# Ten late value slots, dots written in place, earlier value gathers and other releases in a product-key expert layer

## Chip, core and metric

One Trainium2 core runs one decoder layer in one launch. The metric is device time in microseconds (us), median of several runs.

## What is computed

The layer is a hybrid mixer, a memory attention and a product-key expert network; the change touches the last part only.

```python
def peer_ffn(h, w_query, sub_keys, expert_u, expert_v):     # h: 256 tokens x 2048
    q = (h @ w_query).reshape(B, S, 8, 2, 128)
    scores = jnp.einsum('bshcd,hckd->bshck', q, sub_keys)    # 8 heads, 2 x 128 keys
    s_top, i_top = lax.top_k(scores, 16)                     # per half
    cand = s_top[..., 0, :, None] + s_top[..., 1, None, :]   # 16 x 16 pairs
    best, pos = lax.top_k(cand, 16)                          # 16 experts of 16384
    gate = softmax(best)
    act = gelu(einsum('ckd,cd->ck', expert_u[idx], x))       # a dot with each u row
    out = einsum('ck,ckd->cd', gate * act, expert_v[idx])    # weighted sum of v rows
```

The output is the root-mean-square norm of the sum, times `final_norm`. A row of `expert_u` or `expert_v` has 2048 float32, 8 KB.

## The kernel before

Up to about 740 us the kernel runs the mixer, the attention and the query product, weights split into high and low parts. The expert part then works in 16 groups of 128 tokens and one head (groups 0 to 7 are the first 128 tokens, 8 to 15 the second), 16 experts each, so that a gather brings one row to each of the 128 partitions (1 MB).

- **u gathers** (`gather_u`, L566, GpSimd's queue): gather n = 16 g + k. Four slots `u_ring` serve groups 0 and 1; from group 2 on there are seven, with `u_mid` (slots 4, 5) in the place of the query product's input and `u_high` (slot 6) in that of its output. Their first use waits for the last scores (`scores_ready`); later ones wait for the dot that used the slot.
- **Dots** (`dot_products`, L1373 and L1375, VectorE): two halves of 1024 elements each, product written to a bf16 scratch tile `product`, sum to `dots`. Before each stands a wait for the dot before it. Between the dots of group g VectorE does the routing of group g + 1 (`route_keys`, which first copies the scores to `cur`, `route_pairs`, `route_experts`) and, in groups 8 to 15, one-hot tiles for the scattered weights.
- **Value gathers of the first 128 tokens** (`first_values`, L573): 128 gathers v n in a ring of four slots, 4 behind group 1's u gathers, then 6 a group, 12 a group from group 8, 8 in the last two. TensorE takes them (`take_values`, L1875) with a diagonal of weights from ScalarE and counts `v_used`. The first take stands behind the last scores.
- **Dense tiles**: value rows of the upper 48 of 128 key blocks aren't gathered but multiplied from contiguous tiles of 1 MB (SyncE L503, slots 0 to 2 of `u_ring`; TensorE L1910, eight products for each half of the tokens per tile) with weights `wT` that one-hot products scatter (`scatter_weights`, L1904, `wT_done`). The last two heads' values are gathered whole, all others skip the rows that tiles hold. TensorE runs tile 0, then the last take of the first 128 tokens, which frees v slot 3, then tiles 1 to 47.
- **Late gathers** (L573): 128 value gathers m of the second 128 tokens, behind the last u gather on GpSimd's queue. `late_slot(m)` gives the slot: nine at first (7 = `late_first`, 8 = `late_third`, in the place later used by `final_gain`), then seven in turn. VectorE adds them up (`add_values`, L1407, counter `v_added`); six of the last 16 are left to TensorE (`take_late`, L1884), which comes to them after the tiles.

Each engine runs its queue in order, so a wait holds all that stands behind it. SyncE's queue holds the tiles, the load of `final_gain` after tile 8, and the output.

Of the kernel before, what the change touches and what calls it, by code (L numbers as in the profile page):

```python
# [33 lines left out]
def hybrid_layer(  # L34
# [8 lines left out]
    P = 128  # L43
# [13 lines left out]
    TOP = 16  # L57
# [99 lines left out]
    VS = 4  # L157
    V2S = 9
    late_first = put("late_first", [P, 1, D], F32, at_t2)
    late_third = put("late_third", [P, 1, D], F32, at_t1 + 24 * KB)  # L160
    wT = (put("wT0", [P, DENSE, P], F32, at_raw), put("wT1", [P, DENSE, P], F32, at_v))
# [3 lines left out]
    hotA = put("hotA", [P, 2, WB, P], F32, at_raw + 24 * KB)  # L165
    product = put("product", [P, D], BF16, at_f + 16 * KB)
    y_sum = put("y_sum", [P, TT, D], F32, at_t2)
# [27 lines left out]

    cur = put("cur", [P, 2, KEYS], F32, at_f + 8 * KB)
    rest = put("rest", [P, 2, KEYS], F32, at_f + 9 * KB)
# [27 lines left out]
    with ExitStack() as ctx:  # L225
# [108 lines left out]
        def v_slot(i):  # L334

            if i >= 7:
                return (late_first, late_third)[i - 7][:, 0, :]
            return v_parts[i // 2][:, i % 2, :]
# [65 lines left out]

        AT_FIRST = (7, 6, 0, 1, 2, 8, 4, 5, 3)
        IN_TURN = (6, 0, 1, 2, 4, 5, 3)

        def late_slot(m):

            return AT_FIRST[m] if m < V2S else IN_TURN[(m - V2S) % len(IN_TURN)]  # L410

# [19 lines left out]
        def _(sp):  # L431
# [66 lines left out]
            for t in range(DENSE):  # L498
                if t < 3:
                    sp.wait_ge(dot_done, last_dot(t) + 1)  # L500
                else:
                    sp.wait_ge(tile_used, t - 2)
                sp.dma_start(u_ring[:, t % 3, :], v_rows[(FROM + t) * KEYS:(FROM + t + 1) * KEYS, :]).then_inc(tile_landed[t % 3], 16)  # L503
                if t == 8:
                    sp.wait_ge(v_added, added_before(AT_FIRST.index(8) + 1))
                    sp.dma_start(final_gain[:, :], final_norm.rearrange("(o d) -> o d", o=1).to_broadcast([P, D])).then_inc(fgain_landed, 16)
# [10 lines left out]
        def _(pool):  # L517
# [40 lines left out]
            def gather_u(p, k):  # L558

                n = p * TOP + k  # L560
                before = u_before(n)
                if before is not None:
                    pool.wait_ge(dot_done, before + 1)
                elif n >= 2 * TOP:
                    pool.wait_ge(scores_ready, ITEMS["peer"][1])
                nc.gpsimd.indirect_dma_start(  # L566
                    out=u_slot(n), out_offset=None, in_=u_rows,
                    in_offset=bass.IndirectOffsetOnAxis(ap=idx[:, p, k:k + 1], axis=0)).then_inc(u_landed[u_index(n)], 16)
# [20 lines left out]

            pool.wait_ge(routed, 2)  # L590
            for k in range(TOP):
                gather_u(1, k)
            for n in v_share(1):
                first_values(n)
            for p in range(2, GROUPS):
# [6 lines left out]
            for m in range(TILE0):  # L602
                slot, before = late_slot(m), late_before(m)
                if before is not None and by_pe(before):
                    pool.wait_ge(v_used, late_turn(before) + 1)
                elif before is not None:
                    pool.wait_ge(v_added, added_before(before + 1))
                elif slot < VS:
                    pool.wait_ge(v_used, TILE0 - VS + slot + 1)
                elif slot in (4, 5):  # L610
                    pool.wait_ge(dot_done, GROUPS * TOP)
                else:

                    pool.wait_ge(dot_done, last_dot({6: 6, 7: 4, 8: 3}[slot]) + 1)
# [352 lines left out]
        def _(dve):  # L967
# [329 lines left out]
            def route_keys(g):  # L1297

                c, head = g // PH, g % PH
                step(nc.vector.tensor_copy(cur[:, :, :], scores[:, c, head * (2 * KEYS):(head + 1) * (2 * KEYS)].rearrange("p (a k) -> p a k", a=2)),  # L1300
                     apart=True)
                top16([(cur[:, a, :], rest[:, a, :], top[:, a, :], top_at[:, a, :]) for a in range(2)])

# [61 lines left out]

            def dot_products(g, q, c, ks, first=False):
                for k in ks:
                    n = g * TOP + k
                    dve.wait_ge(u_landed[u_index(n)], 16 * u_turn(n))
                    if not (first and k == 0):  # L1370

                        dve.wait_ge(dot_done, n)
                    nc.vector.tensor_tensor_reduce(out=product[:, 0:D // 2], in0=u_slot(n)[:, 0:D // 2], in1=hn[:, c, 0:D // 2], scale=1.0, scalar=0.0,  # L1373
                                                   op0=ALU.mult, op1=ALU.add, accum_out=dots[:, q, 0, k:k + 1])
                    nc.vector.tensor_tensor_reduce(out=product[:, D // 2:], in0=u_slot(n)[:, D // 2:], in1=hn[:, c, D // 2:], scale=1.0, scalar=0.0,  # L1375
                                                   op0=ALU.mult, op1=ALU.add, accum_out=dots[:, q, 1, k:k + 1]).then_inc(dot_done, 1)
# [83 lines left out]
            route(0)  # L1460
            dot_products(0, 0, 0, range(0, 4), first=True)
            gates(0)
# [514 lines left out]
```

## Time and profile before

| | before |
|---|---|
| median of 3 runs | 2032.69 us (2030.73 to 2033.88) |
| profiled execution | 2036.65 us, its span 2034.7 us |
| busy: TensorE, VectorE, ScalarE, GpSimd | 1781, 1369, 573, 1022 us |
| moved by the software queue (gathers) | 451 MB |
| moved by the hardware queue (weights, tiles) | 195 MB |

Shares over the whole span mix two unlike parts: the dense layers, bound by TensorE, and the expert part. The DMA share is the mean busy share of the core's 16 DMA engines; it can read slightly over 1. Idle time before an operation, in brackets or behind the bar, names what ended it.

### The profile page before, as it was taken

What the parts mean: (1) busy time and instruction counts of PE and PEld (TensorE: products, weight loads), DVE (VectorE), ACT (ScalarE), POOL (GpSimd) and SP (SyncE); (2) the same over time, 40 slices, a digit from 0 to 9 for tenths busy, and PEclk for the clock granted to TensorE, in tenths of its full rate; (3) what the DMA queues carried; (4) which work ended last, traced back from release to release, by engine and by line L of the source; (5) the groups of instructions that cost most, each with busy time, mean ns of one, the idle gap of its engine ahead of it and who ended that gap; (6) DMA issues with size and microseconds to landing.
All of it is one profiled execution on the core that took longest, in us unless ns stands there. A gap on an engine that the chain in (4) does not pass through costs nothing.

```text
span 2034.7 us, 19053 instructions
## 1 busy us (share of the span) xinstructions
PE 1781.4 (88%) x6299; PEld 1126.9 (55%) x6299; DVE 1369.4 (67%) x2205; ACT 573.4 (28%) x1039; POOL 1022.3 (50%) x643
## 2 busy tenths in 40 slices
PE   7999999999999999765655588888887999999996
PEld 6888888888888898522222233344433544444442
DVE  5463453223333348799999988787888887887866
ACT  5345454345443510110011033223314720000001
POOL 4443343444432413466566555564555746776743
PEclk9999999999999999887888899999998989999998
DMA  8986455665546689899999999999999999999997
GB/s 212 241 176 139 151 188 156 190 192 186 171 132 215 190 300 382 328 421 417 416 418 417 413 404 388 412 412 406 403 412 400 392 346 405 382 406 378 387 421 319
DMA packets 157643, 647.29 MB, mean 318 GB/s; under 512 B 25894, under 2 KB 31086, under 8 KB 95598
## 3 DMA queue, kind: packets, MB, share of 16 engines
q0 software_dynamic: 73728, 450.98, 55.0%
q1 hardware_dynamic: 83824, 195.16, 30.7%
q8 instruction: 50, 0.82, 0.2%
q14 instruction: 41, 0.34, 0.0%
HBM read 729.91 MB, written 2.10 MB: 360 GB/s over the span
## 4 chain that ended last, share of the span: by engine, by line
PE 38%; DMA 29%; DVE 19%; issue 7%; POOL 6%; SPq 0%; DVEq 0%; ACT 0%; POOLq 0%
PE acc L1526 10%; PE acc L1528 10%; PE acc L1527 10%; DMA u_ring<-in_peer_u_dram,idx 7%; DMA v_high<-in_peer_v_dram,idx 7%; DVE product L1373 6%; DVE product L1375 6%; DMA v_low<-in_peer_v_dram,idx 6%; DMA v_last<-in_peer_v_dram,idx 5%; PE misc L1875 3%; DVE y_sum L1407 2%; POOL v_high L573 2%; POOL v_low L573 1%; DMA late_first<-in_peer_v_dram,idx 1%; DMA u_mid<-in_peer_u_dram,idx 1%
## 5 line engine op out<-in xcount | busy, mean ns | idle before, releaser
L526 POOL TENSOR_TENSOR w_lo<-raw,w_hi 128x1024 fp32r<-128x1024 f32 x112 | 274.7, 2453 | 424.3 <-ACT w_hi L626 424.0
L1875 PE MATMUL misc<-v_high,diag 128*128 128x512 f32 x512 | 267.8, 673 | 99.4 <-DMA v_high<-in_peer_v_dram,idx 93.4
L1526 PE MATMUL acc<-w_hi,t_hi 128*128 128x512 f32 x896 | 354.7, 396 | 0.0
L1875 PE MATMUL misc<-v_low,diag 128*128 128x512 f32 x512 | 269.3, 678 | 93.3 <-DMA v_low<-in_peer_v_dram,idx 81.3
L1528 PE MATMUL acc<-w_hi,t_lo 128*128 128x512 f32 x896 | 349.3, 390 | 0.0
L1527 PE MATMUL acc<-w_lo,t_hi 128*128 128x512 f32 x896 | 348.7, 389 | 0.0
L974 DVE TENSOR_TENSOR w_lo<-raw,w_hi 128x1024 fp32r<-128x1024 f32 x112 | 152.7, 1363 | 267.1 <-ACT w_hi L626 266.9
L626 ACT ACTIVATE w_hi<-raw 128x1024 fp32r<-128x1024 f32 x224 | 237.0, 1060 | 330.7 <-PE acc L1528 290.2
L566 POOL DMA_INDIRECT u_ring<-in_peer_u_dram,idx x160 | 211.4, 1321 | 196.6 <-DVE dots L1375 139.4
L1373 DVE CUSTOM_DVE_ANT_0 product<-u_ring,hn 128x1024 bf16<-128x1024 f32 x160 | 196.0, 1225 | 70.0 <-DMA u_ring<-in_peer_u_dram,idx 53.8
L1875 PEld LDWEIGHTS misc<-v_low,diag 128*128 128x128 f32 x512 | 106.2, 216 | 246.6 <-issue 127.0
L1875 PEld LDWEIGHTS misc<-v_high,diag 128*128 128x128 f32 x512 | 105.2, 215 | 246.8 <-DMA v_high<-in_peer_v_dram,idx 124.0
L573 POOL DMA_INDIRECT v_low<-in_peer_v_dram,idx x100 | 150.9, 1509 | 113.0 <-PE misc L1875 70.4
L573 POOL DMA_INDIRECT v_high<-in_peer_v_dram,idx x100 | 144.1, 1441 | 120.4 <-PE misc L1875 75.0
L1375 DVE CUSTOM_DVE_ANT_0 product<-u_ring,hn 128x1024 bf16<-128x1024 f32 x160 | 195.6, 1223 | 0.0
L1528 PEld LDWEIGHTS acc<-w_hi,t_lo 128*128 128x128 f32 x896 | 168.2, 188 | 35.8
L1526 PEld LDWEIGHTS acc<-w_hi,t_hi 128*128 128x128 f32 x896 | 168.3, 188 | 33.9
L1527 PEld LDWEIGHTS acc<-w_lo,t_hi 128*128 128x128 f32 x896 | 168.4, 188 | 33.4
L1910 PE MATMUL misc<-u_ring,wT 128*128 128x512 f32 x384 | 176.7, 604 | 2.9 <-DMA u_ring<-in_peer_v_dram 2.3
L1910 PE MATMUL acc<-u_ring,wT 128*128 128x512 f32 x384 | 172.3, 592 | 0.0
L1910 PEld LDWEIGHTS misc<-u_ring,wT 128*128 128x128 f32 x384 | 74.1, 194 | 97.5 <-issue 92.9
L1910 PEld LDWEIGHTS acc<-u_ring,wT 128*128 128x128 f32 x384 | 73.0, 190 | 91.8 <-issue 91.8
(271 smaller groups left out, 2127.4 us busy)
## 6 DMA issues: line engine op xcount, KB each, us to landing
u_ring<-in_peer_v_dram SPq DMA_DIRECT2D x48, 1024.0 KB, 8.9
raw<-in_w_in_dram SPq DMA_DIRECT2D x64, 512.0 KB, 6.9
raw<-in_xattn_wk_dram SPq DMA_DIRECT2D x32, 512.0 KB, 4.7
raw<-in_xattn_wv_dram SPq DMA_DIRECT2D x32, 512.0 KB, 3.9
raw<-in_w_out_dram SPq DMA_DIRECT2D x32, 512.0 KB, 4.5
raw<-in_xattn_wq_dram SPq DMA_DIRECT2D x32, 512.0 KB, 4.7
raw<-in_xattn_wo_dram SPq DMA_DIRECT2D x32, 512.0 KB, 4.9
praw<-in_peer_wq_dram SPq DMA_DIRECT2D x24, 512.0 KB, 7.1
```

Of the source, the lines that this page charges most:

```text
L526: nc.gpsimd.tensor_tensor(w_lo[:, j % RING, :, :], raw[:, j % RING, :, :], w_hi[:, j % RING, :, :].bitcast(F32), ALU.subtract).then_inc(lo ...
L566: nc.gpsimd.indirect_dma_start(out=u_slot(n), out_offset=None, in_=u_rows, in_offset=bass.IndirectOffsetOnAxis(ap=idx[:, p, k:k + 1], axis ...
L573: nc.gpsimd.indirect_dma_start(out=v_slot(slot), out_offset=None, in_=v_rows, in_offset=bass.IndirectOffsetOnAxis(ap=idx[:, n // TOP, n % ...
L626: nc.scalar.activation(w_hi[:, j % RING, :, :], raw[:, j % RING, :, :], ACT.Copy).then_inc(hi_done, 1)
L974: nc.vector.tensor_tensor(w_lo[:, j % RING, :, :], raw[:, j % RING, :, :], w_hi[:, j % RING, :, :].bitcast(F32), ALU.subtract).then_inc(lo ...
L1373: nc.vector.tensor_tensor_reduce(out=product[:, 0:D // 2], in0=u_slot(n)[:, 0:D // 2], in1=hn[:, c, 0:D // 2], scale=1.0, scalar=0.0, op0= ...
L1375: nc.vector.tensor_tensor_reduce(out=product[:, D // 2:], in0=u_slot(n)[:, D // 2:], in1=hn[:, c, D // 2:], scale=1.0, scalar=0.0, op0=ALU ...
L1526: nc.tensor.matmul(o, xh, w_hi[:, s, kk, :], start=first, stop=False)
L1527: nc.tensor.matmul(o, xh, w_lo[:, s, kk, :], start=False, stop=False)
L1528: ins = nc.tensor.matmul(o, xl, w_hi[:, s, kk, :], start=False, stop=last)
L1875: ins = nc.tensor.matmul(o, diag[:, n % 4, :], v_slot(n % VS)[:, i * CW:(i + 1) * CW], start=False, stop=False)
L1910: ins = nc.tensor.matmul(o, wT[c][:, t, :], u_ring[:, t % 3, i * CW:(i + 1) * CW], start=c == 1 and t == 0, stop=c == 0 and t == DENSE - 1)
```

## The change

Seven edits:

1. A tenth late slot, `late_hot`, in the place of `hotA`, free once the last weights are scattered. The first 12 late gathers follow one order, the next 80 run through ten slots, the last 36 through seven.
2. SyncE waits for all 256 dots before tiles 1 and 2 (tile 0 as before), and loads `final_gain` after tile 40, once slot 8 is used for the last time (late sum 86).
3. The first uses of u slots 4 and 5 wait for the last query chunk read by TensorE in place of the last scores.
4. The first four value gathers stand before u gathers 9, 12 and 15 of group 1 in place of behind them.
5. The copy of the scores to `cur` is gone.
6. A dot writes its products as float32 over the u row that it reads.
7. The wait for the dot before stands only in groups 13 to 15.

```diff
@@ tiles
     VS = 4
-    V2S = 9
-    late_first = put("late_first", [P, 1, D], F32, at_t2)
-    late_third = put("late_third", [P, 1, D], F32, at_t1 + 24 * KB)
+    V2S = 10
+    late_more = (put("late_first", [P, 1, D], F32, at_t2), put("late_third", [P, 1, D], F32, at_t1 + 24 * KB),
+                 put("late_hot", [P, 1, D], F32, at_raw + 24 * KB))
-    product = put("product", [P, D], BF16, at_f + 16 * KB)
-    cur = put("cur", [P, 2, KEYS], F32, at_f + 8 * KB)
@@ order of the late slots
-        AT_FIRST = (7, 6, 0, 1, 2, 8, 4, 5, 3)
-        IN_TURN = (6, 0, 1, 2, 4, 5, 3)
+        AT_FIRST = (7, 6, 0, 1, 2, 9, 8, 4, 5, 7, 6, 0)
+        WIDE_TURN = (3, 1, 2, 9, 8, 4, 5, 7, 6, 0)
+        IN_TURN = (3, 1, 2, 4, 5, 6, 0)
+        NARROW = len(AT_FIRST) + 8 * len(WIDE_TURN)
         def late_slot(m):
-            return AT_FIRST[m] if m < V2S else IN_TURN[(m - V2S) % len(IN_TURN)]
+            if m < len(AT_FIRST):
+                return AT_FIRST[m]
+            if m < NARROW:
+                return WIDE_TURN[(m - len(AT_FIRST)) % len(WIDE_TURN)]
+            return IN_TURN[(m - NARROW) % len(IN_TURN)]
@@ SyncE, dense tiles
                 if t < 3:
-                    sp.wait_ge(dot_done, last_dot(t) + 1)
+                    sp.wait_ge(dot_done, last_dot(t) + 1 if t == 0 else GROUPS * TOP)
...
-                if t == 8:
-                    sp.wait_ge(v_added, added_before(AT_FIRST.index(8) + 1))
+                if t == 40:
+                    sp.wait_ge(v_added, added_before(max(m for m in range(TILE0) if late_slot(m) == 8) + 1))
                     sp.dma_start(final_gain[:, :], ...)
@@ GpSimd, gather_u
                     pool.wait_ge(dot_done, before + 1)
+                elif u_index(n) in (4, 5):
+                    pool.wait_ge(peer_used, PC)
                 elif n >= 2 * TOP:
                     pool.wait_ge(scores_ready, ITEMS["peer"][1])
@@ GpSimd, group 1
             for k in range(TOP):
+                if k == 9:
+                    first_values(0)
+                elif k == 12:
+                    first_values(1)
+                elif k == TOP - 1:
+                    first_values(2)
+                    first_values(3)
                 gather_u(1, k)
-            for n in v_share(1):
-                first_values(n)
@@ GpSimd, late gathers
                 elif slot in (4, 5):
                     pool.wait_ge(dot_done, GROUPS * TOP)
+                elif slot == 9:
+                    pool.wait_ge(wT_done, 2 * BATCHES)
@@ VectorE, route_keys
-                step(nc.vector.tensor_copy(cur[:, :, :], scores[...]), apart=True)
-                top16([(cur[:, a, :], rest[:, a, :], top[:, a, :], top_at[:, a, :]) for a in range(2)])
+                top16([(scores[:, c, (2 * head + a) * KEYS:(2 * head + a + 1) * KEYS], rest[:, a, :], top[:, a, :], top_at[:, a, :]) for a in range(2)])
@@ VectorE, dot_products
-                    if not (first and k == 0):
+                    if g >= GROUPS - WHOLE - 1:
                         dve.wait_ge(dot_done, n)
-                    nc.vector.tensor_tensor_reduce(out=product[:, 0:D // 2], in0=u_slot(n)[:, 0:D // 2], ...)
-                    nc.vector.tensor_tensor_reduce(out=product[:, D // 2:], in0=u_slot(n)[:, D // 2:], ...).then_inc(dot_done, 1)
+                    nc.vector.tensor_tensor_reduce(out=row[:, 0:D // 2], in0=row[:, 0:D // 2], ...)
+                    nc.vector.tensor_tensor_reduce(out=row[:, D // 2:], in0=row[:, D // 2:], ...).then_inc(dot_done, 1)
```

## Rows read from the trace of the kernel before

**Rows 1.** Page, DMA queues: packets, MB, share of 16 engines
```profile
q0 software_dynamic: 73728, 450.98, 55.0%
```

**Rows 2.** Windows: us, PE, PEld, DVE, ACT, POOL busy, PEclk, DMA share, GB/s
```profile
785.00:860.00 75.00, 60.28 (x280) 51.14 (x279) 64.44 (x135) 12.37 (x21) 37.99 (x27) 0.89 0.91 335
870.00:880.00 10.00, 5.34 (x12) 1.82 (x10) 8.86 (x30) 0.00 (x0) 6.25 (x7) 0.97 1.02 422
...
855.00:1165.00 310.00, 186.98 (x314) 72.92 (x315) 280.82 (x615) 32.71 (x71) 186.35 (x138) 0.82 1.01 416
...
1165.00:1640.00 475.00, 395.06 (x1187) 193.43 (x1186) 396.19 (x844) 168.99 (x433) 268.76 (x214) 0.94 1.00 403
```

**Rows 3.** Lines, VectorE, 880 to 1160: busy, mean ns | idle before, releasers
```profile
L1373 DVE CUSTOM_DVE_ANT_0 product<-u_ring,hn 128x1024 bf16<-128x1024 f32 x51 | 62.5, 1226 | 9.2 <-DMA u_ring<-in_peer_u_dram,idx 1.3 <-DVE top_at L1295 1.0 <-DVE pos L1295 1.0
```

**Rows 4.** Timeline of VectorE: start, us, operation; group 2's copy, two dots
```profile
773.30 0.29 DVE L1300 COPY cur<-scores 128x256 f32<-128x256 f32 x1
773.74 0.49 DVE L1290 MAX8 top<-cur 128x8 f32<-128x128 f32 x2
...
1004.84 1.23 DVE L1373 CUSTOM_DVE_ANT_0 product<-u_mid,hn 128x1024 bf16<-128x1024 f32 x1
...
1005.99 1.22 DVE L1375 CUSTOM_DVE_ANT_0 product<-u_mid,hn 128x1024 bf16<-128x1024 f32 x1
...
1007.36 1.23 DVE L1373 CUSTOM_DVE_ANT_0 product<-u_high,hn 128x1024 bf16<-128x1024 f32 x1
```

**Rows 5.** Timeline of GpSimd, first value gathers; idle before in brackets
```profile
848.88 1.01 POOL L573 DMA_INDIRECT v_low<-in_peer_v_dram,idx  x1 [0.30 <-issue]
...
855.66 1.56 POOL L566 DMA_INDIRECT u_mid<-in_peer_u_dram,idx  x1 [0.77 <-ACT scores L927]
...
862.14 1.00 POOL L573 DMA_INDIRECT v_low<-in_peer_v_dram,idx  x1 [2.06 <-PE misc L1875]
```

**Rows 6.** Timeline of ScalarE, group 2's exponentials
```profile
849.01 0.31 ACT L827 ACTIVATE exps<-best,neg_best 128x16 f32<-128x16 f32 x1 [22.75 <-DVE neg_best L1313]
```

**Rows 7.** Windows of the tail, same columns as rows 2
```profile
1640.00:1660.00 20.00, 17.96 (x59) 10.26 (x58) 12.12 (x16) 6.59 (x16) 4.65 (x5) 0.83 0.91 362
1660.00:1680.00 20.00, 20.00 (x48) 8.78 (x47) 19.24 (x11) 0.99 (x3) 14.72 (x7) 1.00 0.84 301
1700.00:1920.00 220.00, 220.00 (x514) 97.42 (x513) 177.85 (x76) 0.00 (x0) 154.40 (x77) 1.00 0.99 389
```

**Rows 8.** Timeline of GpSimd, late gathers 5, 8, 9 and 126
```profile
1651.06 1.00 POOL L573 DMA_INDIRECT late_third<-in_peer_v_dram,idx  x1 [6.04 <-DVE dots L1375]
...
1663.32 1.82 POOL L573 DMA_INDIRECT v_high<-in_peer_v_dram,idx  x1 [8.65 <-PE misc L1875]
1665.44 2.15 POOL L573 DMA_INDIRECT v_last<-in_peer_v_dram,idx  x1 [0.30 <-issue]
...
2006.08 2.59 POOL L573 DMA_INDIRECT v_more<-in_peer_v_dram,idx  x1 [1.31 <-PE acc L1884]
```

**Rows 9.** Timeline of TensorE: last query chunks, tiles 0 and 1, first take
```profile
822.46 13.98 PE L1855 MATMUL acc<-t2f,praw 128*128 128x256 f32 x64
...
1649.81 5.85 PE L1910 MATMUL misc<-u_ring,wT 128*128 128x512 f32 x8 [0.58 <-ACT wT L849]
...
1662.36 3.60 PE L1910 MATMUL misc<-u_ring,wT 128*128 128x512 f32 x8
...
1989.55 3.60 PE L1884 MATMUL acc<-v_high,diag 128*128 128x512 f32 x8
```

**Rows 10.** Last lines of the sources L503 (dense tiles) and L573 (value gathers)
```profile
DMA to landing us min/median/max: 8.0/8.9/10.8
...
DMA to landing us min/median/max: 5.8/16.2/27.6
```

**Rows 11.** Timeline of VectorE, second halves of dots 253 and 255
```profile
1638.56 1.22 DVE L1375 CUSTOM_DVE_ANT_0 product<-u_ring,hn 128x1024 bf16<-128x1024 f32 x1
...
1649.04 1.22 DVE L1375 CUSTOM_DVE_ANT_0 product<-u_ring,hn 128x1024 bf16<-128x1024 f32 x1
```

More of the change, by code:

```diff
@@ L336, in v_slot @@
             if i >= 7:
-                return (late_first, late_third)[i - 7][:, 0, :]
+                return late_more[i - 7][:, 0, :]
             return v_parts[i // 2][:, i % 2, :]
@@ L590, in _ @@
             pool.wait_ge(routed, 2)
+            assert FIRST_V == 4
             for k in range(TOP):
+                if k == 9:
[5 more added lines that the diff above has]
+                    first_values(3)
                 gather_u(1, k)
-            for n in v_share(1):
-                first_values(n)
             for p in range(2, GROUPS):
@@ L1299, in route_keys @@
                 c, head = g // PH, g % PH
-                step(nc.vector.tensor_copy(cur[:, :, :], scores[:, c, head * (2 * KEYS):(head + 1) * (2 * KEYS)].rearrange("p (a k) -> p a k", a=2)),
-                     apart=True)
-                top16([(cur[:, a, :], rest[:, a, :], top[:, a, :], top_at[:, a, :]) for a in range(2)])
+                top16([(scores[:, c, (2 * head + a) * KEYS:(2 * head + a + 1) * KEYS], rest[:, a, :], top[:, a, :], top_at[:, a, :]) for a in range(2)])
             def route_pairs(g):
@@ L1364, in one_hots, with dot_products @@
                                         ALU.mult).then_inc(hot_ready, 1)
-            def dot_products(g, q, c, ks, first=False):
+            def dot_products(g, q, c, ks):
                 for k in ks:
                     n = g * TOP + k
+                    row = u_slot(n)
                     dve.wait_ge(u_landed[u_index(n)], 16 * u_turn(n))
-                    if not (first and k == 0):
+                    if g >= GROUPS - WHOLE - 1:
                         dve.wait_ge(dot_done, n)
-                    nc.vector.tensor_tensor_reduce(out=product[:, 0:D // 2], in0=u_slot(n)[:, 0:D // 2], in1=hn[:, c, 0:D // 2], scale=1.0, scalar=0.0,
+                    nc.vector.tensor_tensor_reduce(out=row[:, 0:D // 2], in0=row[:, 0:D // 2], in1=hn[:, c, 0:D // 2], scale=1.0, scalar=0.0,
                                                    op0=ALU.mult, op1=ALU.add, accum_out=dots[:, q, 0, k:k + 1])
-                    nc.vector.tensor_tensor_reduce(out=product[:, D // 2:], in0=u_slot(n)[:, D // 2:], in1=hn[:, c, D // 2:], scale=1.0, scalar=0.0,
+                    nc.vector.tensor_tensor_reduce(out=row[:, D // 2:], in0=row[:, D // 2:], in1=hn[:, c, D // 2:], scale=1.0, scalar=0.0,
                                                    op0=ALU.mult, op1=ALU.add, accum_out=dots[:, q, 1, k:k + 1]).then_inc(dot_done, 1)
@@ L1460, in _ @@
             route(0)
-            dot_products(0, 0, 0, range(0, 4), first=True)
+            dot_products(0, 0, 0, range(0, 4))
             gates(0)
```

## The prediction, made before the changed kernel ran

> **What bounds the kernel now.** I read the page's slices first, to see where the DMA line goes to nines and stays: from about 740 us, where the expert part begins. Before it lie the dense layers, which nothing in the diff touches. Windows then split the expert part in four [rows 2, 7]. In each the reader should look at the DMA share: it stands at 1.01 to 1.02 when the queues never run dry, so what is missing to 1.015 is time in which a transfer could have run and did not.
>
> - Start, 785 to 860: share 0.91, hence 0.105 x 75 = 7.9 us unused [rows 2].
> - Groups 2 to 7, 855 to 1165: share 1.01, 416 GB/s, but VectorE is busy 281 of 310 us [rows 2], and before a dot it waits for a transfer only 1.3 us over 51 dots [rows 3]. Both are at their limit.
> - Groups 8 to 15, 1165 to 1640: share 1.00, so 0.015 x 475 = 7 us unused, VectorE with slack [rows 2].
> - Tail: 1640 to 1680 misses (0.105 + 0.175) x 20 = 5.6 us, 1700 to 1920 misses 0.025 x 220 = 5.5 us [rows 7]. TensorE is busy all the time here: its dense tiles run without a break from 1649.8 to 1989.6 [rows 9].
>
> Size of a gather: a u gather is 1.049 MB. The software queue moved 450.98 MB [rows 1]; less 256 u gathers and the 32 v gathers of the last two heads, 288 x 1.049 = 302 MB, that leaves 149 MB for 224 v gathers, 0.665 MB each, 1.6 us at 416 GB/s.
>
> **Part by part.**
>
> *Copy into `cur` gone.* The COPY starts at 773.30 and the MAX8 behind it at 773.74 [rows 4]: 0.44 us of VectorE per group. In group 0 it lies on the path to the very first gather: -0.4 us. Reading `scores` in its place has the same shape and type: 0.
>
> *Dots in place, no pause in groups 0 to 12.* From L1373 to the L1375 behind it, with no wait between, VectorE takes 1.15 us; from L1375 over the wait to the next dot 1.37 us [rows 4]. So a pause costs 0.22 us. Eleven of a group's 16 dots (1, 3, 5, 7 to 9, 11 to 15) follow a dot directly (behind the others stand steps with waits of their own): 2.4 us per group, with the copy 2.9. The output changes from bf16 to f32; no row has this operation with f32 output. Bounds: 0 (a rate of one element a cycle is already what 1.15 us for 1024 elements means) and, above, the whole 1.15 us again if an f32 row took two passes. I take 0, since the L1407 sums, f32 out of two inputs, keep about 1.2 us per 1024 too (GpSimd, held to their pace, starts a gather after the 2.15 us of the one before and a 0.30 us gap, 2.45 us for 2048 elements [rows 8]).
> What it is worth: groups 2 to 7 take 50.4 us each (310 us hold 129 MB, so 21.0 MB a group). VectorE would need 47.5, the queues at 420 GB/s (they did 422 in [rows 2]) 49.9. So transfers are next late and only 0.5 us a group is gained: -2.5 us over six groups, between 0 (416 GB/s is already the ceiling) and -4. Groups 8 to 12 wait for transfers already: -1, between 0 and -4.
> The Trainium skill, "VectorE: DVE Perf Modes", section "The DRAIN you can't avoid", says that chaining Vector operations without semaphores saves nothing. The rows speak against it with 1.15 against 1.37 us. By that rule groups 2 to 7 would stay bound by VectorE at 50.4 - 0.44 = 50.0 us, and the sum would be only about 1 us smaller.
>
> *First values among group 1's u gathers.* Today the four gathers start at 848.9, behind u gather 15 [rows 5]; in the change they are spread from about 822 to 844. Their 2.7 MB (6.4 us) go into the 7.9 us unused there. But GpSimd then meets the next lock: v gather 4 waits for TensorE's first take, at 862.1 [rows 5], and behind it stand u gathers 35 and on. The take waits for the scores, done at 854.9, whose last step ScalarE starts late, as it stood behind the exponentials of group 2 at 849.0 [rows 6]. That does not move with the gathers. So from 850 on only u 31 to 34, 3.8 MB or 9 us, are in flight, and the queues are short of work for 3 to 4 us before 864. Net 6.4 - 3.5 = -3, plus what VectorE brings group 2's routing forward (two copies, two pauses, 1.3 us): -4. Bounds: -1.5 and -7.9. The v gathers share bandwidth with u gathers 24 to 30; VectorE is busy 64 of 75 us in 785 to 860 [rows 2], so a transfer 1.6 us later mostly finds it at routing; cost 0, at most 1.6. The waits on `peer_used` before v 0 and v 2 ask for 20 and 32 chunks; TensorE has read the 32nd at 836.4 [rows 9], ahead of v 2's place, and the 20th half an item and more sooner: cost 0 (without that cover u 25 or u 31 would stand behind the wait).
>
> *Middle slots by the query weights.* Today u 32 and 33 are issued at 855.7, released by the scores [rows 5]. With only the routing to wait for they go at about 850.5. It is this that keeps the queues fed from 850 to 860; it is in the -4 already. Slot 6 still waits for the scores.
>
> *Ten late slots.* After the last dot, at 1650.3 [rows 11], GpSimd issues three gathers and is blocked until 1663.3, when TensorE frees v slot 3 [rows 8]; that is the hole of [rows 7]. The new order puts the tenth slot (free when TensorE has scattered the last weights, about 1649.3) and three second uses of slots 7, 6, 0 (freed by the first three sums, which follow the last dot at 2.455 us each) ahead of slot 3: four more gathers, 2.7 MB or 6.5 us, against a hole of 5.6: -5.6, between -3 and -5.6. From there to late gather 92 ten are in flight in place of seven: of 5.5 us unused I take -3 (0 to -5.5). After that, seven as before.
>
> *Tiles 1 and 2 wait for all dots.* SyncE sends tile 1 after dot 253, whose second half starts at 1638.56 [rows 11]; that is at 1639.8, now after dot 255 at 1650.3: 10.5 us later; tile 2 about 5 us later, and the tiles behind them in order. TensorE wants tile 1 at 1662.4 [rows 9], 12.1 us after the new issue. A tile lands in 8.0 to 10.8 us [rows 10], but here two start together, 2.1 MB beside the gathers' stream, 10 to 13 us. Cost 0 to +3 on TensorE; I take +1. Their 2 MB leave the full stretch before 1650 and go into the hole; that is no gain of its own.
>
> *Final gain behind tile 40.* SyncE now waits there for late sum 86 (slot 8's last). Late gather 9 went at 1665.4 and 126 at 2006.1 [rows 8], so 86 near 1890; with 16.2 us to land [rows 10] and the sum, 1908. Tile 41 is due when TensorE has done tile 38, (1989.6 - 1662.4) / 47 = 6.96 us each, at 1927: cost 0 with 19 us to spare. If that cover were gone, each us late would be one on TensorE.
>
> *What then ends last.* TensorE's takes of late values begin at 1989.6 [rows 9], and each frees a slot: late gather 126 needs the fourth, 1989.6 + 4 x 3.43 = 2003.3, and went at 2006.1 [rows 8]. In a full queue a v gather lands in 16.2 us [rows 10]; the last four, 4.2 MB, need no less than 10. So the tail can gain 2.8 + 6.2 = 9 at most, whatever the slots do; its parts, -5.6 - 3 + 1 = -7.6, stay under it.
>
> **Sum.** -0.4 - 4 - 2.5 - 1 - 7.6 = -15.5 us. The profiled execution took 2036.65 us (span 2034.7), 4.0 over the median; so it would be 2021.2, and the median 2032.7 - 15.5 = **2017.2**.
>
> **Rivals.**
>
> *Transfers were already at their ceiling.* 416 GB/s in groups 2 to 7 is all there is, the holes elsewhere only move, ten slots find no unused time: -0.4 - 2 - 3 (part of the hole) = -5.5, **2027**. For it: share 1.01. Against: two clear holes.
>
> *More than the sum.* The start gives its whole 6.4 us, the groups 8, the tail its 9: -0.4 - 6.4 - 8 - 9 = -24, **2009**. For it: faster dots shorten the loop dot, gather, dot everywhere. Against: GpSimd's lock at 862.
>
> *GpSimd starved by unpaused dots: slower.* A gather issued beside a running VectorE operation finishes only after that one's end: in the tail each takes 2.15 us and goes at VectorE's pace, 2.455 us [rows 8], against 1.0 us alone [rows 5]. Without the pause nothing but the seam between two operations lets it in. In groups 2 to 7 GpSimd's mean is 186/138 = 1.35 us [rows 2], 22 gathers a group, 36 us. It decides from (49.9/22) - 0.3 = 1.97 us (0.3 is the gap between two gathers [rows 5]). At 2.15 us a group costs 22 x 2.45 = 53.9, +3.5 each, and groups 8 to 12, 28 gathers, 68.6 against 59.4, +9 each: 21 + 46 less the other gains, 12: +55, **2088**. Against: L1373 to L1375 is such a seam without a wait, and gathers pass at it (the u gather at 855.7 took 1.56 us [rows 5]). The Trainium skill, "SBUF — State Buffer", section "Who interferes with whom", says that a Vector operation with two SBUF inputs locks the shared port against GpSimd's reads for its whole length; the ticking at 2.455 us agrees.
>
> *Same as before, or mislaid.* Tiles late enough to make TensorE stall 5 us and more while the start gives 1: about -2, **2031**.
>
> **Chances.** Forecast (2012 to 2023) 0.55; ceiling (2023 to 2028.6) 0.2; more than the sum 0.12; about unchanged 0.06; starved 0.07 (from a few us up). 0.2% is 4.1 us, about what can be told apart here. Faster 0.87, same 0.06, slower 0.07. The range, leaving out the tail of "more" and both last cases: **2006 to 2028**.
>
> **What would show it.** Right: L1375 to L1373 at 1.15 us in groups 0 to 12; VectorE with waits for transfers in groups 2 to 7; DMA share near 1.0 in 785 to 850, then a dip before 864; group 8 reached about 7 us earlier; share 1.0 in the 40 us after the last dot; late gathers landing 7 us sooner than the rest of the shift. Wrong: GpSimd gathers above 1.97 us in the mean; dots longer than 1.23 us; TensorE waiting for tile 1 by more than 3 us, or tile 41 waiting for the gain.

## Result and profile after

The changed kernel takes 2021.45 us (median, 2019.40 to 2022.96), beside 2032.58 us of the kernel before: ratio 0.9938, interval 0.9927 to 0.9950. That is 11.1 us faster by the medians, where 15.5 were forecast (2017.2).

The two profiled executions lie 17.3 us apart by their spans (2034.7 and 2017.4), since the one of before was a long one of its kernel and this one a short one. A second profile of the changed kernel (2020.1) stands beside it below. Marks along the way:

| | before | after | after, again | forecast of the step |
|---|---|---|---|---|
| first dot | 747.9 | 747.5 | 748.3 | -0.4 |
| first dot of group 2 | 864.5 | 855.5 | 855.5 | -4.4 so far |
| first dot of group 8 | 1170.5 | 1162.0 | 1163.6 | -2.5 more |
| end of the last dot | 1650.3 | 1638.9 | 1640.8 | -1 more |
| end | 2034.7 | 2017.4 | 2020.1 | -7.6 more |
| from last dot to end | 384.4 | 378.5 | 379.3 | -7.6 |

By these marks the start gave 9 us in place of 4.4, groups 2 to 7 nothing in place of 2.5, groups 8 to 15 about 3 in place of 1, the tail 5 to 6 in place of 7.6. Together that is 14.6 to 17.3 us, more than the 11.1 of the times, and the excess has a likely place. The only profile of the kernel before was 4.1 us over its median. A second execution of the same code up to the first value gather exists, in the run with lighter gathers further down, and it is 4.1 us earlier at the last u gather of group 1:

```profile
846.65 1.93 POOL L566 DMA_INDIRECT u_ring<-in_peer_u_dram,idx  x1 [4.85 <-DVE dots L1375]
```

```profile
842.58 1.92 POOL L566 DMA_INDIRECT u_ring<-in_peer_u_dram,idx  x1 [4.85 <-DVE dots L1377]
```

The first line is the kernel before, the second that run. With these 4.1 us taken off, the start gave 4.9 us, and the whole 10.5 to 13.2. So of the 9 us in the table about 5 are safe; between 5 and 9 the profiles do not decide.

The windows of the changed kernel, columns and stretches as in [rows 2, 7]:

```profile
785.00:860.00 75.00, 65.57 (x298) 53.83 (x297) 66.69 (x139) 14.45 (x24) 39.55 (x30) 0.93 0.99 384
855.00:1165.00 310.00, 191.65 (x312) 74.27 (x310) 277.92 (x611) 30.95 (x68) 190.24 (x139) 0.80 1.01 415
1165.00:1640.00 475.00, 397.22 (x1216) 197.82 (x1217) 393.81 (x837) 174.04 (x443) 274.00 (x213) 0.94 0.99 403
1640.00:1660.00 20.00, 20.00 (x46) 8.71 (x45) 19.23 (x11) 1.95 (x5) 17.48 (x9) 0.96 0.99 395
1660.00:1680.00 20.00, 20.00 (x48) 8.88 (x47) 17.25 (x8) 0.00 (x0) 17.56 (x9) 1.00 1.01 413
1700.00:1920.00 220.00, 220.00 (x514) 97.33 (x513) 184.35 (x80) 0.00 (x0) 160.18 (x78) 1.00 0.99 395
```

The DMA share of the start rose from 0.91 to 0.99, at 384 in place of 335 GB/s. In groups 2 to 7 it stands where it stood, at 415 in place of 416 GB/s: this is the stage in which nothing was gained. The hole behind the last dot is mostly closed.

Two dots in a row, VectorE's timeline, which answers to [rows 4]:

```profile
846.70 1.22 DVE L1386 CUSTOM_DVE_ANT_0 u_ring<-u_ring,hn 128x1024 f32<-128x1024 f32 x1
847.84 1.22 DVE L1388 CUSTOM_DVE_ANT_0 u_ring<-u_ring,hn 128x1024 f32<-128x1024 f32 x1
848.99 1.22 DVE L1386 CUSTOM_DVE_ANT_0 u_ring<-u_ring,hn 128x1024 f32<-128x1024 f32 x1
```

From L1388 over no wait to the next L1386 it is 1.15 us, as from L1386 to L1388; it was 1.37. The f32 product costs nothing (1.22 us an operation, as with bf16). What VectorE gained it now spends waiting, as the lines of VectorE in 880 to 1160 show (see [rows 3]):

```profile
L1386 DVE CUSTOM_DVE_ANT_0 u_ring<-u_ring,hn 128x1024 f32<-128x1024 f32 x51 | 62.3, 1222 | 11.5 <-DMA u_ring<-in_peer_u_dram,idx 9.5 <-DVE top_at L1309 0.7 <-DVE pos L1309 0.6
```

9.5 us of waiting for transfers over 51 dots where it was 1.3.

The first value gathers on GpSimd's timeline (see [rows 5]), and ScalarE's exponentials (see [rows 6]):

```profile
817.98 1.04 POOL L579 DMA_INDIRECT v_low<-in_peer_v_dram,idx  x1 [0.30 <-issue]
...
826.07 1.88 POOL L579 DMA_INDIRECT v_low<-in_peer_v_dram,idx  x1 [0.31 <-issue]
...
839.10 1.00 POOL L579 DMA_INDIRECT v_high<-in_peer_v_dram,idx  x1 [0.30 <-issue]
...
847.05 1.70 POOL L572 DMA_INDIRECT u_mid<-in_peer_u_dram,idx  x1 [3.20 <-DVE idx L1336]
...
855.47 1.01 POOL L579 DMA_INDIRECT v_low<-in_peer_v_dram,idx  x1 [3.19 <-PE misc L1888]
```

```profile
844.28 0.31 ACT L841 ACTIVATE exps<-best,neg_best 128x16 f32<-128x16 f32 x1 [17.46 <-DVE neg_best L1325]
```

All went as laid out, none of the first four value gathers (0 to 3; the last row is value gather 4) waits, and u 32 goes at 847.05 with the routing. But the whole pattern lies 3 to 5 us earlier than the working had it: the exponentials at 844.3, where 849.0 less 1.3 was expected, and value gather 4 at 855.5 in place of about 861.

Behind the last dot, GpSimd and TensorE (see [rows 8, 9]):

```profile
1633.61 1.00 POOL L579 DMA_INDIRECT v_high<-in_peer_v_dram,idx  x1 [5.75 <-PE misc L1888]
1638.78 1.00 POOL L579 DMA_INDIRECT late_hot<-in_peer_v_dram,idx  x1 [4.17 <-PE acc L1917]
...
1647.47 2.26 POOL L579 DMA_INDIRECT late_first<-in_peer_v_dram,idx  x1 [0.31 <-issue]
...
1654.94 2.15 POOL L579 DMA_INDIRECT v_high<-in_peer_v_dram,idx  x1 [0.31 <-issue]
```

```profile
1638.57 5.23 PE L1923 MATMUL misc<-u_ring,wT 128*128 128x512 f32 x8 [0.58 <-ACT wT L863]
...
1650.50 3.60 PE L1923 MATMUL misc<-u_ring,wT 128*128 128x512 f32 x8
...
1977.59 7.03 PE L1897 MATMUL acc<-v_high,diag 128*128 128x512 f32 x16
```

From 1638.78 on the gathers follow one another without a gap but 0.3 us, where there was a pause of 8.65 us. Tile 1 starts 11.9 us behind tile 0 (12.6 before), without a wait: the later issue of tiles 1 and 2 cost nothing. The chain that ended last now runs over TensorE's tiles through nearly all of the tail; over the whole span TensorE's part rose from 38% to 61%.

### The profile page after: what moved, and what is told of

Its sections match the earlier page's. It is cut to its first block, busy times and chain, and to the rows that moved or that the text cites. A ratio compares the mean times of both kernels' runs of the same rounds, so it can differ in the third digit from the quotient of the medians.

```text
span 2017.4 us, 18828 instructions
## 1 busy us (share of the span) xinstructions
PE 1782.3 (88%) x6299; PEld 1128.2 (56%) x6299; DVE 1360.8 (67%) x2189; ACT 574.2 (28%) x1039; POOL 1035.0 (51%) x643
## 4 chain that ended last, share of the span: by engine, by line
PE 61%; DMA 19%; DVE 13%; issue 4%; POOL 3%; ACT 1%; SPq 0%; DVEq 0%; POOLq 0%; ACTq 0%
PE acc L1539 10%; PE acc L1541 10%; PE acc L1540 10%; PE acc L1923 8%; PE misc L1923 8%; DMA v_high<-in_peer_v_dram,idx 6%; DMA u_ring<-in_peer_u_dram,idx 6%; PE misc L1888 4%; PE acc L1868 3%; DVE u_ring L1388 2%; DVE u_ring L1386 2%; DMA v_low<-in_peer_v_dram,idx 2%; DMA u_high<-in_peer_u_dram,idx 2%; PE acc L1829 1%; DVE u_mid L1388 1%
## 5 line engine op out<-in xcount | busy, mean ns | idle before, releaser
L1888 PE MATMUL misc<-v_high,diag 128*128 128x512 f32 x512 | 275.4, 690 | 100.0 <-DMA v_high<-in_peer_v_dram,idx 95.5
L572 POOL DMA_INDIRECT u_ring<-in_peer_u_dram,idx x160 | 207.3, 1295 | 183.4 <-DVE dots L1388 122.9
L1386 DVE CUSTOM_DVE_ANT_0 u_ring<-u_ring,hn 128x1024 f32<-128x1024 f32 x160 | 195.7, 1223 | 69.3 <-DMA u_ring<-in_peer_u_dram,idx 62.6
L1388 DVE CUSTOM_DVE_ANT_0 u_ring<-u_ring,hn 128x1024 f32<-128x1024 f32 x160 | 195.7, 1223 | 0.0
L579 POOL DMA_INDIRECT v_low<-in_peer_v_dram,idx x93 | 134.7, 1448 | 92.3 <-PE misc L1888 55.5
```

What stands on the lines that cost most here:

```text
L572: nc.gpsimd.indirect_dma_start(out=u_slot(n), out_offset=None, in_=u_rows, in_offset=bass.IndirectOffsetOnAxis(ap=idx[:, p, k:k + 1], axis ...
L579: nc.gpsimd.indirect_dma_start(out=v_slot(slot), out_offset=None, in_=v_rows, in_offset=bass.IndirectOffsetOnAxis(ap=idx[:, n // TOP, n % ...
L1386: nc.vector.tensor_tensor_reduce(out=row[:, 0:D // 2], in0=row[:, 0:D // 2], in1=hn[:, c, 0:D // 2], scale=1.0, scalar=0.0, op0=ALU.mult, ...
L1388: nc.vector.tensor_tensor_reduce(out=row[:, D // 2:], in0=row[:, D // 2:], in1=hn[:, c, D // 2:], scale=1.0, scalar=0.0, op0=ALU.mult, op1 ...
L1888: ins = nc.tensor.matmul(o, diag[:, n % 4, :], v_slot(n % VS)[:, i * CW:(i + 1) * CW], start=False, stop=False)
```

## Experiments

All but the single executions were timed beside the kernel before on the same chip, in three rounds on three chips, where the kernel before took 2033.4, 2034.7 and 2036.4 us. So ratios are compared across rounds, not times. Their intervals are 0.14% to 0.29% (3 to 6 us) to either side; the interval of every variant of the changed kernel overlaps the changed kernel's own, and a single edit of 2 to 6 us is not resolved by the time of the whole.

The readings therefore rest on marks within profiles, and these scatter too. Five kernels below have the same code up to group 2 (the changed one twice, nine slots, no wait at all, TensorE relieved): group 2's first dot is at 855.5, 855.5, 856.2, 853.8 and 857.4 us. Four of them have the same code to shortly before the last dot, which ends at 1638.9, 1640.8, 1641.2 and 1646.3. Groups 2 to 7 take 305.3 to 311.0 us in the ten profiles with full gathers and no wait between these groups' dots. A mark inside such a spread shows nothing.

**The changed kernel again.**

> The changed kernel again, as the measure for the runs beside it. Expected 11 to 13 us under the kernel before (2020 to 2022 us), group 2's first dot near 855.5 us in its profile and the last dot's end near 1639.

2021.6 us, ratio 0.9945 (0.9927 to 0.9964). The marks are in the table above.

**Wait before every dot.**

```diff
-                    if g >= GROUPS - WHOLE - 1:
+                    if n:
                         dve.wait_ge(dot_done, n)
```

> The changed kernel with the wait before every dot, dots still in place. Theory (a pause counts where a dot gates the next gather, so in groups 0 and 1 with four slots, and not where the queues are full): L1388 to the next L1386 back at 1.37 us; group 2's first dot 3 to 5 us later than in the changed kernel, groups 2 to 7 as long as before (50.4 to 51 us each), the whole 3 to 6 us slower than the changed kernel. Rival A (transfers are the only bound everywhere): no difference beyond 2 us. Rival B (faster dots carry most of the gain): 8 us or more slower.

2026.6 us (median), 5 us over the changed kernel in the same round, ratio 0.9954 (0.9938 to 0.9970) beside 0.9945 (0.9927 to 0.9964). Group 2's first dot at 859.0, +3.5; groups 2 to 7 take 310.0 us against 306.5 and 308.1; last dot 1647.7, +7 to +9. The dots' spacing is back:

```profile
1004.73 1.22 DVE L1387 CUSTOM_DVE_ANT_0 u_high<-u_high,hn 128x1024 f32<-128x1024 f32 x1
...
1006.10 1.23 DVE L1385 CUSTOM_DVE_ANT_0 u_ring<-u_ring,hn 128x1024 f32<-128x1024 f32 x1
```

1.37 us. Group 2's first dot lies 1.6 us behind the latest of the five profiles without the pause, so an effect in the start is likely, as the theory has it, but of one profile. The 310.0 us of groups 2 to 7 lie inside the spread of 305.3 to 311.0, and the last dot only 1.4 us behind the latest: beyond the start no effect is shown. The 5 us speak against rival A's 2 us, without ruling it out, as the intervals overlap; rival B's 8 us aren't reached.

**The dots' edits alone, on the kernel before.** No copy, product in place, wait in groups 13 to 15 only.

> The kernel before with the dots' edits alone: no copy, products written in place, no wait between dots in groups 0 to 12. Theory from the runs so far (the wait put back cost 5 us in the changed kernel; these edits gate the four-slot loop of groups 0 and 1 and lift VectorE's bound in groups 2 to 7): group 2's first dot about 3.5 to 4 us earlier than before (861), last dot 5 to 8 us earlier, the whole 4 to 7 us under the kernel before. Rival (it pays only together with the earlier gathers): 0 to 2 us.

Ratio 0.9963 (0.9949 to 0.9977), 7 us by the medians. Group 2's first dot at 862.3, -2.1, less than the 3.5 expected and less than the 4.1 us by which the kernel before differs from itself; groups 2 to 7 306.1 us against 306.0: nothing. The last dot 3.9 us earlier, and from there to the end 381.1 us against 384.4, which no edit of this run explains. The dots' edits thus pay alone, by the times; at which place the profiles don't show, nor whether they pay more together with the gathers.

**Start put back: both edits, the gathers alone, the slots alone.**

```diff
             for k in range(TOP):
-                if k == 9:
-                    first_values(0)
...
                 gather_u(1, k)
+            for n in v_share(1):
+                first_values(n)
```

```diff
-                elif u_index(n) in (4, 5):
-                    pool.wait_ge(peer_used, PC)
```

> The changed kernel with the first four value gathers behind group 1's u gathers and u slots 4 and 5 released by the scores, as before. Theory (these two give half of the 9 us by which group 2 starts earlier): group 2's first dot 4 to 5 us later, near 860, the whole 3 to 5 us slower. Rival (faster dots give nearly all of the start): within 2 us.

> The changed kernel with only the first four value gathers put back behind group 1's u gathers; u slots 4 and 5 still go with the query weights. Theory (it is the place of the gathers that fills the start; undoing both edits moved group 2's first dot by 5 us): the first value gather behind u 31, DMA share in 785 to 850 back from 0.99 to about 0.93, u 32 issued behind four more gathers, group 2's first dot 3 to 5 us later (859 to 861), the whole 3 to 5 us slower than the changed kernel. Rival (the earlier release of the slots alone is enough): group 2's first dot within 1.5 us.

> The changed kernel with only the release of u slots 4 and 5 put back to the scores. Theory: the routing is there at 846.6 and the scores at 850.2, so u 32 goes 3.5 us later, group 2's first dot 2 to 3.5 us later, the whole 0 to 3 us slower, as groups 2 to 7 are bound by transfers and GpSimd is held by the first take at 855 anyway. Rival (this edit carries the 5 us): 4 us or more slower.

Group 2's first dot: 860.7 with both undone (+5.2), 860.4 with the gathers back (+4.9), 856.5 with the slots back (+1.0, where 2 to 3.5 were expected, and inside the spread). Whole, by the ratio: 0.9953, 0.9944, 0.9945, beside 0.9938 and 0.9945 of the changed kernel; no difference is resolved. The window of 785 to 850, of the changed kernel and then of the one with the gathers back, columns as in [rows 2]:

```profile
785.00:850.00 65.00, 55.77 (x273) 49.34 (x271) 58.04 (x122) 9.47 (x15) 33.65 (x26) 0.92 0.99 388
```

```profile
785.00:850.00 65.00, 55.87 (x273) 49.43 (x271) 57.85 (x122) 9.26 (x15) 35.01 (x24) 0.92 0.94 356
```

The share falls from 0.99 to 0.94 when the gathers are put back (0.93 with both undone, 0.99 to 1.00 in the five profiles with the new place); with only the slots put back it is 0.97, at 384 GB/s. The gathers' place carries what these two edits give, the release of the two slots 1 us at most that could be seen, as the scores follow the routing by 3 us and GpSimd comes to the first take soon after in any case.

**Scores ahead of the exponentials on ScalarE.**

```diff
-            gate_exp(2)
             evacuate_queries(items - 1)
             peer_scores(items)
+            gate_exp(2)
```

> The changed kernel with one order changed on ScalarE: the copy of the last query product and the last scores stand ahead of group 2's exponentials. Theory (TensorE has the query product ready at 837 and ScalarE begins on it only at 844.6, so the first take and value gather 4 behind it come 7 us late): scores about 843, first take about 844 to 846, value gather 4 issued near 849 in place of 855.5, u 34 with u 32 and 33; DMA share 840 to 870 from 0.97 to 1.01, group 3 to 8 begin 1 to 2.5 us earlier, the whole 1 to 3 us faster than the changed kernel. Rival (the queues hold enough work until 855): within 1 us.

2019.6 us, ratio 0.9924 (0.9895 to 0.9953), the lowest median of all, but not told apart from the changed kernel, and the expected way isn't the one it took. The scores were done at 840.5, ten us earlier, yet TensorE's first take began at 847.4 and value gather 4 went at 854.8 (855.5 before the edit):

```profile
849.30 1.70 POOL L572 DMA_INDIRECT u_mid<-in_peer_u_dram,idx  x1 [3.20 <-DVE idx L1336]
...
854.83 1.26 POOL L579 DMA_INDIRECT v_low<-in_peer_v_dram,idx  x1 [0.30 <-issue]
```

GpSimd isn't held by TensorE any longer, only by the routing, and the routing was 2.3 us later in this run. That is not the edit's doing: VectorE began on it at 830.4 against 828.1, before the moved steps, the first of which ran at 836.7. From u gather 32 to value gather 4 it is 5.5 us against 8.4, so 2.9 of the 3.2 us for which GpSimd waits there in the changed kernel are gone. What that is worth in the end isn't shown: group 3 began at 908.8, no earlier than in the changed kernel (906.5 and 909.1), with the late routing in it. Next in line, at 849.3, is the routing on VectorE.

**Lighter transfers in groups 2 to 7, in both kernels.** One execution each.

```diff
                 last = FROM * KEYS - 1 if n // TOP < GROUPS - WHOLE else KEYS * KEYS - 1
+                if n < 40:
+                    last = KEYS * KEYS // 4 - 1
```

> The kernel before, with value gathers 0 to 39 (those of groups 1 to 7) bounded at a quarter of the value table in place of five eighths, so each moves about 0.26 MB in place of 0.66 and most of their rows are left out: less to move in groups 2 to 7, same work on VectorE. Theory (in the kernel before VectorE needed all of its 50.4 us per group there and the transfers nearly as much): groups 3 to 7 stay at 50 to 50.6 us each, DMA share falls to about 0.93. Rival (transfers alone set the pace): 45 to 47 us each.

> The changed kernel with the same lighter value gathers 0 to 39, most of their rows left out. Theory (dots are faster by 2.9 us a group but transfers were at their ceiling, which hid it): with the transfers out of the way groups 3 to 7 take 47 to 48.3 us each, 2.4 to 3 less than in the kernel before with the same gathers. Rival (the saved pauses come back elsewhere on VectorE): 50 us, as in the kernel before.

In the kernel before, groups 2 to 7 take 302.2 us, 50.4 each, against 306.0 and 51.0 with the full gathers. In the changed one they take 283.5 us, 47.3 each, against 306.5 and 51.1. A window inside that stage, first before, then changed:

```profile
900.00:1100.00 200.00, 112.34 (x197) 44.44 (x195) 185.79 (x406) 20.10 (x44) 119.30 (x88) 0.80 0.95 371
```

```profile
900.00:1100.00 200.00, 123.73 (x209) 48.36 (x208) 192.12 (x438) 22.29 (x48) 137.83 (x95) 0.82 0.99 399
```

With 371 GB/s the old kernel leaves the queues partly unused and is only 0.6 us a group faster: VectorE sets its pace, and in 908 to 1110 it never waits for a transfer. The new one is 3.1 us a group faster than the old one, where 2.9 was worked out, and waits 0.4 us in all for transfers in 903 to 1091. Both rivals fall; the 23 us are far outside any spread. So the changed VectorE could run a group in 47.3 us; with the full gathers the transfers hold it at 51.1. This pair is the firmest result here: the edits of the dots do what was worked out, and the transfers hide it.

**Nine slots and the old order.**

```diff
-        AT_FIRST = (7, 6, 0, 1, 2, 9, 8, 4, 5, 7, 6, 0)
-        WIDE_TURN = (3, 1, 2, 9, 8, 4, 5, 7, 6, 0)
-        IN_TURN = (3, 1, 2, 4, 5, 6, 0)
+        AT_FIRST = (7, 6, 0, 1, 2, 8, 4, 5, 3)
+        WIDE_TURN = ()
+        IN_TURN = (6, 0, 1, 2, 4, 5, 3)
```

> The changed kernel with the nine slots and the order of the kernel before. Theory (the hole after the last dot and the unused time in the tail were worth about 6 us): last dot as in the changed kernel, the hole after it back (DMA share about 0.85 in the 30 us behind the last dot), 4 to 8 us slower than the changed kernel. Rival (TensorE's tiles, unbroken from the first, set the end, so slots bring nothing): within 2 us of the changed kernel.

2027.6 us by the median, 6 over the changed kernel in the same round; last dot at 1641.2 as there, then 385.6 us to the end against 378.5 and 379.3. The 30 us behind the last dot and 200 us of the tail, first the changed kernel (second profile), then nine slots:

```profile
1641.00:1671.00 30.00, 30.00 (x64) 12.86 (x63) 27.00 (x14) 2.78 (x6) 26.34 (x13) 0.91 0.97 382
1700.00:1900.00 200.00, 200.00 (x467) 88.54 (x466) 171.49 (x74) 0.00 (x0) 151.53 (x72) 1.00 0.99 394
```

```profile
1641.00:1671.00 30.00, 30.00 (x63) 13.05 (x64) 26.66 (x17) 2.78 (x6) 20.79 (x10) 0.90 0.90 331
1700.00:1900.00 200.00, 200.00 (x467) 88.54 (x466) 163.48 (x70) 0.00 (x0) 150.40 (x70) 1.00 0.98 386
```

The share behind the last dot is 0.90 where about 0.85 was expected. Over all profiles the stretch from last dot to end is 377.2 to 380.4 us in the nine with ten slots (mean 378.7; TensorE relieved left out) and 381.1 to 385.6 in the four with nine (before, this one, the dots alone, the lighter gathers before; mean 383.9). Number and order of the slots together are worth 5 us; the order of the last 36 gathers differs too and was not tested by itself. In unused time the 5 us stand in two places: (0.97 - 0.90) x 30 = 2.1 us behind the last dot, and 8 of 394 GB/s over 200 us, 4 us. Against the kernel before, whose share in 1650 to 1680 is 0.83 and whose rate in 1700 to 1900 is 388 GB/s, the same two are (0.97 - 0.83) x 30 = 4.2 us and 6 of 394 GB/s, 3 us; together they are 1 to 2 us more than the stretch got shorter.

Where the gain comes out is another matter. TensorE's tiles run without a break, and from the last dot to its first take of a late value, behind the tiles, it is 336.2 to 339.3 us with nine slots and 337.0 to 339.9 with ten: the hole behind the last dot costs nothing there. From that take to the end it is 44.9 to 47.1 us with nine and 39.8 to 42.2 with ten. The takes of the changed kernel (second profile) and of this one:

```profile
1979.18 7.03 PE L1897 MATMUL acc<-v_high,diag 128*128 128x512 f32 x16
...
1999.72 3.70 PE L1897 MATMUL acc<-v_more,diag 128*128 128x512 f32 x8 [1.38 <-DMA v_more<-in_peer_v_dram,idx]
```

```profile
1979.73 3.60 PE L1897 MATMUL acc<-v_high,diag 128*128 128x512 f32 x8
...
2001.18 5.40 PE L1897 MATMUL acc<-v_last,diag 128*128 128x512 f32 x8 [3.98 <-DMA v_last<-in_peer_v_dram,idx]
```

So filled holes pay only as late gathers that no longer stand behind the tiles: eight are issued there in place of nine. More tail can be had only from these 40 us or from TensorE's 338.

**No wait between dots at all.** The condition on `g` taken away.

> The changed kernel without any wait between dots, the last three groups too. Theory (groups 13 to 15 are bound by transfers and by the ring of value slots, VectorE has slack): last dot 0 to 2 us earlier, whole within 2 us. Rival (unpaused dots keep GpSimd from the shared port, and that is why the wait stays in the last three groups): mean of a gather in the last three groups 0.2 us or more above the changed kernel's, last dot 3 us or more later.

The rival holds in part: 2025.9 us, ratio 0.9954 (0.9939 to 0.9970), not resolved from the changed kernel's. Up to group 14 nothing moves (1528.3 against 1527.9); the last dot then comes at 1644.0 (1638.9, 1640.8). From group 14's first dot it is 115.7 us, against 112.6 to 113.4 in the four profiles that keep the wait and are alike up to there. The last three groups, changed kernel (second profile), then without waits:

```profile
1460.00:1640.00 180.00, 148.39 (x529) 80.29 (x527) 153.40 (x315) 81.39 (x208) 107.53 (x77) 0.94 1.00 406
```

```profile
1460.00:1640.00 180.00, 151.58 (x504) 79.86 (x502) 150.75 (x311) 80.95 (x206) 117.16 (x77) 0.91 0.97 393
```

The fifth pair is GpSimd: 117.2 us for 77 gathers against 107.5 for 77, 1.52 against 1.40 us each (0.12 where the rival asked for 0.2), and the DMA share falls from 1.00 to 0.97. The mean hides what happens. GpSimd's timeline in group 14, without waits:

```profile
1561.48 5.28 POOL L572 DMA_INDIRECT u_ring<-in_peer_u_dram,idx  x1 [0.30 <-issue]
1567.07 5.80 POOL L572 DMA_INDIRECT u_ring<-in_peer_u_dram,idx  x1 [0.31 <-issue]
1573.17 5.40 POOL L579 DMA_INDIRECT v_high<-in_peer_v_dram,idx  x1 [0.30 <-issue]
```

These three gathers take 16.5 us, while VectorE goes through dots and one-hot operations with hardly a gap; the longest gather of the changed kernel in that stretch takes 3.4 us. In 1530 to 1582 the share is 0.87 against 1.00. So the mechanism of the slower rival is real, in bursts. One-hot operations between unpaused dots alone don't make it: groups 8 to 12 have both in the changed kernel, and the mean in 1165 to 1465 is 1.23 us, against 1.20 with the waits back. What else it takes isn't shown.

**TensorE relieved in the tail.** One execution.

```diff
-                    dense_tile(t, 1).then_inc(tile_used, 1)
+                    (ins if t % 2 else dense_tile(t, 1)).then_inc(tile_used, 1)
```

> The changed kernel with the second tokens' half of every second dense tile left out (24 of 48, so part of the output of the second 128 tokens is missing): TensorE has 12 x 6.87 = 82 us less to do in the tail, the same tiles and gathers are loaded. Theory (the tail's end is set by transfers, TensorE is 4 us short of setting it): tiles come no faster than transfers bring them, DMA share in the tail 1.0 with tiles drawing a larger part, end 0 to 6 us earlier than the changed kernel. Rival (TensorE's unbroken tiles set the end): 10 us or more earlier.

Both missed: the span is 2034.9 us, and the stretch from last dot to end 388.6, 10 us longer. SyncE's timeline and TensorE's waits tell why:

```profile
1848.08 3.76 SPq L507 DMA_DIRECT2D u_ring<-in_peer_v_dram  x2
1916.53 0.33 SPq L510 DMA_DIRECT2D final_gain<-in_final_norm_dram  x1
```

```profile
PE misc L1923 <- DMA u_ring<-in_peer_v_dram: 60.5, 5, 57.6
```

Faster tiles brought SyncE to tile 40 at 1852, 65 us before late sum 86 was done (1916.5), and TensorE stood still for 57.6 us behind the wait for the gain's place. In the changed kernel the sum ends at 1881.0 and tile 41 is sent at 1911.6, so 31 us are spare. The wait is free only as long as the sums stay ahead of the tiles. How much the tail would shrink with less work on TensorE and no such wait this run can't say; it stays open.

## Why the prediction came out as it did

The sign, the range and the order of size held: -15.5 forecast, -11.1 measured by the times. The closeness is in part luck. Two terms were too small and two too large; by the profiles they add up to -14.6 to -17.3, or -10.5 to -13.2 with the 4.1 us of the one profile of before taken off.

- **Copy and pause: right.** 1.15 us against 1.37, no cost of f32 or of writing in place, 3.1 us a group when transfers are out of the way (2.9 forecast). The rule of the Trainium skill that the prediction cites ("VectorE: DVE Perf Modes", section "The DRAIN you can't avoid"), that chaining Vector operations without semaphores saves nothing, doesn't hold for these operations.
- **Start: -9 by the marks for -4.4, but -4.9 with the 4.1 us taken off.** The prediction had "only u 31 to 34, 3.8 MB or 9 us, are in flight"; four u gathers are 4.2 MB. Put back one at a time, the place of the gathers moved group 2's first dot by 4.9 us, where the working had 3 net. Of the slots the prediction said "it is this that keeps the queues fed"; putting their release back moved the mark by 1.0 us and left the share at 0.97, so that was too much. The step "two copies, two pauses, 1.3 us" counted pauses only along the routing of group 2. Groups 0 and 1 run in four slots, so a dot gates the gather four on; putting the waits back moved group 2 by 3.5 us. Both steps, of one profile each, speak for more than 4.9 us together; whether it was 5 or 9 stays open. The lock at the first take was priced at 3.5 us; GpSimd waits 3.2 us there, and what this costs the whole isn't shown.
- **Groups 2 to 7: mechanism right, worth 0 for -2.5.** The step that failed is the 420 GB/s of full queues, taken from one window of 10 us. In 855 to 1165 the profiles of full gathers run at 410 to 417, before and after; the rival of the ceiling was right for this stage. The working was off in two small ways too: a group of the kernel before takes 51.0 us by the marks, not 50.4, and six times 0.5 is 3.0.
- **Groups 8 to 15: -2.6 to -2.9 for -1**, inside its bounds. Which edit brings it isn't settled; the dots alone give 1.8 (479.8 to 478.0 us).
- **Tail: -5.1 to -5.9 for -7.6.** The parts were priced as unused transfer time: hole behind the last dot -4.2 for -5.6, ten slots behind it -3 for -3. But time filled there doesn't shorten TensorE's 338 us of tiles; it comes out behind them, where the prediction had its limit of 9, and less of it. GpSimd also waits ahead of the dot's end, at 1628 to 1638.8, for TensorE's takes and for the tenth slot, which no part of the working had. Tiles 1 and 2: 0 for +1. Final gain: 0, right, with 31 us of cover for the 19 worked out.
- **Starved GpSimd:** did not decide in groups 2 to 7 (mean 190/139 = 1.37 us after 1.35, the edge was put at 1.97), but with the wait taken from the last three groups too it does, in a burst of group 14. The change keeps the wait there.

## What to carry to other kernels

Before a stage's gain is read from two profiles, look how far the same code differs from itself: here by 4.1 us in the start and by up to 7.4 at the last dot. Where a short ring of buffers makes gathers wait for an engine, the place to fill other transfers in is among these gathers. Where queues and engine are both full, relieve one and look for the other: lighten the transfers in both versions to see whether the engine's gain is there at all. Unused transfer time is worth only what ends later because of it, so price it at the engine that ends last. A wait that is free because another queue is slow should be noted with its margin, since the next improvement can turn it into a lock.

## What was not expected of the hardware

- A wait on the semaphore that the operation just before raises costs VectorE 0.22 us between two 128x1024 operations (1.37 against 1.15 us from start to start).
- Without the pause GpSimd's mean gather in groups 2 to 7 stays what it was (1.37 us after 1.35), though VectorE's dots then follow one another with no wait; in the last three groups it costs 0.12 us per gather, nearly all of it in three gathers of 5.3 to 5.8 us.
- With the DMA share at 0.98 to 1.01 throughout, the rate is 410 to 417 GB/s in groups 2 to 7, where 6 of 22 gathers are bounded (their skipped rows move nothing), 398 to 405 in groups 8 to 15 with their many bounded ones, and 386 to 397 in the tail. That skipped rows still take DMA time would explain it. The lighter gathers, which skip more rows, point the same way: the rate divided by the share in 900 to 1100 falls from 413 to 391 GB/s in the kernel before (371 at 0.95) and from 415 to 403 in the changed one (399 at 0.99). What one skipped row takes no run measured.
